# Down stage, first pair: the g blocks of the fifth, sixth and seventh product are loaded three to four units later and split later

## The reference

```
h2 = rmsnorm(x, ffn_pre_g)
up = causal_depthwise_conv(h2 @ w_up, conv_f_w, conv_f_b)
u_gate, u_val = split(up, 2)
f = (gelu(u_gate) * u_val) @ w_down
x = x + rmsnorm(f, ffn_post_g)
```

## Time and profile before

| | |
|---|---|
| median of 3 runs | 2552.38 us (2551.55 to 2552.54) |
| profiled execution | 2550.99 us |
| its span | 2549.2 us |
| TensorE busy | 2512.1 us, 99% |
| VectorE busy | 1839.5 us, 72% |
| ScalarE busy | 1021.6 us, 40% |
| first pair of the down stage | from 1892.6 us |

### The profile page before, as it was taken

How to read it: one execution, slowest core, us unless ns; L and a number is a source line. 1 busy time by engine, 2 the same in 40 slices (tenths; PEclk the granted TensorE clock), 3 DMA queues, 4 the chain that set the end, 5 groups by cost and what they waited for, 6 DMA issues and landing times. The chain is left out here.

```text
span 2549.2 us, 36122 instructions
## 1 busy us (share of the span) xinstructions
PE 2512.1 (99%) x14276; PEld 2207.3 (87%) x14276; DVE 1839.5 (72%) x2226; ACT 1021.6 (40%) x1199; POOL 184.7 (7%) x261
## 2 busy tenths in 40 slices
PE   9999999999999999999999999999999999999998
PEld 7788888888888888899999999999987878877886
DVE  7888766653334236889899998999988787888434
ACT  5222322252223224444444444444454453455323
POOL 0000000000000000011111111111111111200000
PEclk9999999999999999999999999999999999999999
DMA  4332323233233423567777777777787777976221
GB/s 170 104 103 91 105 94 99 91 116 96 94 99 108 149 98 128 157 178 221 207 189 215 207 220 200 197 217 204 219 272 243 256 245 190 270 235 227 89 98 68
DMA packets 153554, 418.71 MB, mean 164 GB/s; under 512 B 12992, under 2 KB 46784, under 8 KB 152384
## 3 DMA queue, kind: packets, MB, share of 16 engines
q1 hardware_dynamic: 120080, 293.64, 33.6%
q0 software_dynamic: 30928, 118.50, 19.4%
q10 hardware_dynamic: 2400, 4.53, 0.5%
HBM read 379.66 MB, written 36.96 MB: 163 GB/s over the span
## 5 line engine op out<-in xcount | busy, mean ns | idle before, releaser
L1082 ACT ACTIVATE w_hi<-ring_raw 128x1024 fp32r<-128x1024 f32 x426 | 450.3, 1060 | 603.1 <-PE ps L980 389.7
L1504 DVE TENSOR_TENSOR ring_lo<-ring_raw,w_hi 128x1024 fp32r<-128x1024 f32 x426 | 518.3, 1221 | 189.8 <-ACT w_hi L1082 188.4
L1493 DVE TENSOR_TENSOR w_lo<-w_raw,w_hi 128x1024 fp32r<-128x1024 f32 x192 | 234.4, 1224 | 405.2 <-ACT w_hi L1072 404.9
L1072 ACT ACTIVATE w_hi<-w_raw 128x1024 fp32r<-128x1024 f32 x192 | 202.6, 1059 | 515.4 <-PE ps L760 366.0
L758 PE MATMUL ps<-xg_hi,w_hi 128*128 128x512 f32 x1024 | 400.7, 391 | 4.9 <-DVE w_lo L1493 3.3
L759 PE MATMUL ps<-xg_lo,w_hi 128*128 128x512 f32 x1024 | 399.1, 390 | 0.0
L760 PE MATMUL ps<-xg_hi,w_lo 128*128 128x512 f32 x1024 | 399.0, 390 | 0.0
L978 PE MATMUL ps<-s_hi,w_hi 128*128 128x256 f32 x1280 | 361.4, 282 | 2.5 <-issue 2.4
L980 PE MATMUL ps<-s_hi,ring_lo 128*128 128x256 f32 x1280 | 361.7, 283 | 0.0
L979 PE MATMUL ps<-s_lo,w_hi 128*128 128x256 f32 x1280 | 361.2, 282 | 0.0
L978 PE MATMUL ps<-xg_hi,w_hi 128*128 128x256 f32 x960 | 271.0, 282 | 2.3 <-DVE ring_lo L1504 2.3
(11 more groups left out here) (248 smaller groups left out, 4206.3 us busy)
## 6 DMA issues: line engine op xcount, KB each, us to landing
ring_raw<-in_w_up SPq DMA_DIRECT2D x200, 512.0 KB, 4.9
ring_raw<-in_w_down SPq DMA_DIRECT2D x114, 512.0 KB, 5.1
w_raw<-in_w_in SPq DMA_DIRECT2D x110, 512.0 KB, 3.3
ring_raw<-in_w_up POOLq DMA_DIRECT2D x80, 512.0 KB, 6.3
w_raw<-in_w_o SPq DMA_DIRECT2D x32, 512.0 KB, 3.6
ring_raw<-in_w_ple_gate SPq DMA_DIRECT2D x32, 512.0 KB, 3.6
xd_raw<-gx_dram POOLq DMA_DIRECT2D x14, 1024.0 KB, 11.0
gx_dram<-g_sums POOLq DMA_DIRECT2D x44, 256.0 KB, 9.1
```

The lines of the kernel that those rows point to most:

```text
L1082: f(w_hi[:, (U_S + n) % SLOTS], raw_of(n), ACT.Copy).then_inc(hi_ready, 1)
L1493: dve.tensor_tensor(w_lo[:, s], w_raw[:, u.slot(RAW)], as_f32(w_hi[:, s]), ALU.subtract).then_inc(lo_ready, 1)
L1504: dve.tensor_tensor(low_of_unit(n), raw_of(n), as_f32(w_hi[:, (U_S + n) % SLOTS]), ALU.subtract).then_inc(lo_ready, 1)
```

## The change

Three loads are issued after units 9, 12 and 14 in place of 6, 8 and 10, and the preparation of the same three products stands in the loop at positions 13, 16 and 19 in place of 11, 13 and 18. Nothing else is changed.

```diff
@@ -438,7 +438,7 @@
-        PREPARED = {0: (0, T1), 1: (0, T2), 11: (0, W22), 13: (0, W21), 18: (0, T4)}
+        PREPARED = {0: (0, T1), 1: (0, T2), 13: (0, W22), 16: (0, W21), 19: (0, T4)}
@@ -686,12 +686,12 @@
-                if i == 6:
+                if i == 9:
                     pool.wait_ge(gx_out[0], g_stored(QUADS - 1))
                     load_blocks(0, W22)
-                if i == 8:
+                if i == 12:
                     load_blocks(0, W21)
-                if i == 10:
+                if i == 14:
                     load_blocks(0, T4)
```

## The result

The changed kernel takes 2556.4 us (median of 19 runs, 2553.57 to 2559.22), the kernel before 2551.33 us beside it (19 runs, 2548.74 to 2553.35). The ratio is 1.002 with a 95% interval of 1.0013 to 1.0026, so +5.1 us (+3.3 to +6.6). The forecast was 5.5 us more, 2557.9 us on the earlier median. The measured ratio lies on the line of 0.2% itself, and its interval reaches to both sides of it.

The account below looks back on a forecast made before the run. TensorE, busy 2512.1 of 2549.2 us, was taken to bound the kernel. 4.1 us of later start at unit 21 plus 1.4 us of clock made 5.5 us, giving 2557.9 us from the 2552.38 us median; range 2555.0 to 2561.0 us.

Parts of the forecast that it names:

- Who waits: Before unit 21, TensorE's 1.97 us idle, named "issue" in the view, ends with T4's low half made on VectorE.
- The loads: Three block loads issued later in the first down-stage pair: cost 0 if landings stay below 11.5 us; gain 0 to 0.3 us.
- W22: Halves moved from position 11 to 13: unit 16 starts 0.1 us late, taken back later; cost 0, bounds 0 and 0.2 us.
- W21: Halves moved from position 13 to 16, behind VectorE's takes: unit 20 waits 0.9 us, counted inside the 4.1 us.
- T4: Halves moved from position 18 to 19: low half ends at 1964.4 us, so unit 21 starts 4.1 us later.
- Given back: After unit 21, to the end of the stage: later waits move along, so nothing is recovered; bound 0.5 us.
- The clock: Behind the new stops at units 20 and 21: one drop to half clock costs 1.4 us, bounds 0 and 2.8 us.

Follow-up runs that it names:

- the filled kernel: The changed kernel with 16 small matmuls of constants, read by nothing, put on TensorE ahead of unit 21: 2554.86 us, ratio 1.0013 to the kernel before.
- the kernel with the old loads: The changed kernel with its three loads back after units 6, 8 and 10, preparation still at 13, 16 and 19: 2556.71 us, ratio 1.0022 to before.
- the kernel that is faster up to unit 23: The kernel before with W22, W21 and T4 prepared at positions 10, 12 and 13, loads as before: 2547.5 us, ratio 0.9986.
- T4 at 18: The changed kernel with only T4's preparation back at position 18, W22 and W21 still at 13 and 16: 2552.33 us, ratio 1.0005 to before.
- the one with added matmuls ahead of unit 4: The kernel before with preparation at 10, 12 and 13, plus 8 and 7 constant matmuls ahead of units 4 and 5: 2549.37 us, ratio 0.9989.

## Why the prediction was right, point by point

- **Who waits.** "What is it waiting for? Its blocks": right. The half ends 0.10 us before unit 21 in the changed kernel too, and the filled kernel has the name in the trace.
- **The loads.** Taken at 0: right, by the kernel with the old loads (0.04 us of difference to the end of the stage). The landing times of 8.6 to 10.0 us that I carried over were too long for the profiled run, 6.2 to 8.2 us; in the three other kernels with late loads they are 6.9 to 9.9 us. This only widened a margin.
- **W22.** Expected 0.1 us, bound 0.2: the trace shows a start that waited (0.47 us in place of 0.39 us); it stands 0.04 us behind the old one (1944.90 less 0.25 against 1944.61 us).
- **W21.** Expected unit 20 0.9 us late: it is 1956.64 less 0.25 less 1955.49, 0.9 us.
- **T4.** Expected 4.1 us, measured 4.07 us, in two parts that add up.
- **Given back.** Taken at 0 with a bound of 0.5 us: right within that bound. The clock's loss is over by unit 23, which starts here in the kernel before and in the changed one:

```profile
1966.01 0.39 PE L1024 MATMUL ps<-w_hi,xd 128*128 128x512 f32 x1
```

```profile
1972.96 0.39 PE L1024 MATMUL ps<-w_hi,xd 128*128 128x512 f32 x1
```

From unit 7 that is 6.70 us more, and 6.51 us more at the end of the stage, so 0.2 us came back. The waits behind the earlier trace rows are these in the changed kernel:

```profile
PE ps L1024 <- DVE cb L2159: 1.3, 2, 1.0
...
PE ps L1024 <- DVE ring_lo L1504: 0.5, 2, 0.3
```

In the kernel with the old loads nothing came back (6.43 us at unit 23, 6.47 at the end), in the filled one 0.45 us (4.04 and 3.59), and the kernel that is faster up to unit 23 gains another 0.26 us behind it (-2.25 and -2.51). So these tenths vary from trace to trace, and do not follow what was lost.
- **The clock.** One drop of 1.4 us was added, bounds 0 and 2.8. This is the term that the runs bear out least. In the trace the difference grows from 4.07 us at unit 21 to 6.70 us at unit 23, so the drop cost 2.6 us, near the upper bound, and 2.4 us in the kernel with the old loads; the filled kernel, with the same order, loses 0.02 us there. The medians say less: 5.1 us less 4.07 us is 1.0 us, and 1.5 us against the filled kernel. The mean granted clock, recorded for every run, is 0.9961 over the 19 runs of the changed kernel, and 0.9968 and 0.9971 over the 32 and 27 runs of the kernel before. Times 2556 us that is about 2 to 3 us of full clock more that was held back, some of it while TensorE stood still (an estimate from means of values rounded to 0.001). So as a mean the cost seems to lie between 1 and 2 us, and 1.4 us was not far off; in both traces of this stop it was a microsecond or more too low. The drop that the 1.4 us was copied from was itself priced a little low: the matmuls of unit 5 start over 4.18 us there, 1911.69 to 1915.87 us, and over 2.6 us where the clock holds, so it cost 1.6 us.

How far the drop spreads the runs was not measured run by run, and it is not the only thing that does. In the trace with only T4 moved the granted clock is also 0.50 from 1092.5 to 1095 us, where no edit reaches.

The Trainium skill ("TensorE: Matmul & The Clock Gate", Part 1) has the gate at all or half of the pulses by how busy TensorE lately was. The filled kernel agrees: granted clock 1.00 behind the filled stop, 0.50 behind the empty one. The Trainium skill ("DMA: Bandwidth & Descriptors", section "Issuing engines are not separate DMA queues") has all queues on the same 16 engines. The traces agree: in the four kernels with late block loads the weight loads of 1919.5 to 1930 us land in 3.4 to 4.3 us (medians), in the kernel before and the three with early block loads and nothing added on TensorE in 6.5 to 6.9 us. No TensorE wait was there for it to shorten.

The sum of 5.5 us stands against 5.1 us, with 3.3 to 6.6 us as its interval, which does not tell the two apart. The 4.1 us of order is shown to a tenth. That the total came so near is in part luck, since the one drop of clock was taken over from another stop, and the stage is 6.5 us longer in the profiled pair.

## What to carry to other kernels

A prepared operand has two ends: the landing it needs and the engine that prepares it. Before a preparation is moved, write out that engine's row of work up to the point where the operand is wanted; a place just before a burst of other duties (here four takes after a product ends) is worth several microseconds more than the same place just behind it. If the consumer is the bottleneck and the preparing engine has pauses earlier, put it there: here T4's half at position 19 belongs to a loss of 5 us, and at position 13 to a gain of over 2 us. And count a stop on TensorE together with the slow stretch that may follow it, as a range and not as one number.

## What the runs showed of the hardware that was not expected

- The low clock behind a stop differs: behind a stop of 2.58 us it was low for 3.3 us, behind 3.11 us for 3.4 us, behind 4.45 us for 4.6 us, behind 5.08 us for 5.5 us, and not at all behind 1.97 us before unit 21 or behind 5 us of which 3.73 us were filled with matmuls that nothing uses. From unit 21 to unit 23 that cost 1.4, 1.6, 2.2 and 2.6 us.
- The length of the stop does not decide alone. Before units 4 and 5 TensorE stands still for 0.82 and 1.96 us with only T4 moved, and for 0.83 and 2.20 us with T4 at 18. Behind the second stop the clock is low in the first of these kernels (0.56 from 1911.6 to 1915.0 us) and not in the other (1.00 from 1909.9 to 1914.6 us). Unit 5 in each:

```profile
1909.94 0.47 PE L1024 MATMUL ps<-w_hi,xd 128*128 128x512 f32 x1 [1.96 <-DVE ring_lo L1504]
```

```profile
1910.00 0.47 PE L1024 MATMUL ps<-w_hi,xd 128*128 128x512 f32 x1 [2.20 <-DVE ring_lo L1504]
```

- A block load of 1 MB is not clearly quicker for being issued 9 to 11 us later: the first of the three landed in 6.9 to 7.6 us in the four kernels with late loads and in 7.7 to 10.3 us in the five with early ones, the third in 8.2 to 9.9 us and in 7.8 to 9.0 us. The weight loads beside them are what landed sooner.
- The landing of the weights at the start of the stage varies from run to run: ScalarE's wait for it was 2.9 to 5.2 us in the eight traces with nothing changed before it, and 7.4 us in the one with added matmuls ahead of unit 4. TensorE's start of unit 4 moves with it.
